# Centred norms of a two-block transformer kernel: the second tile's squares in two halves about the first half's mean

## The chip, the core and the metric

The kernel runs on one core of a Trainium2 chip. The core has a matmul engine (TensorE, PE), a vector engine (VectorE, DVE), an activation engine (ScalarE, ACT), a general engine (GpSimd, POOL) and a queue engine that issues DMAs (SyncE, SP). Each engine takes its own instructions in order; they meet only through semaphores. The metric is the device time of one execution in microseconds (us), lower is better.

## What is computed

Two model blocks on 256 tokens of width 1024, all in float32: a hybrid block (gated convolution and 16-head attention, between two RMS norms), then a two-layer block with memory attention, a sparse attention, another attention and two feed-forward nets. In the second block every sublayer ends in a layer norm of the scaled input plus the sublayer's output. It is this norm that the change touches:

```python
def layer_norm(x, g, b):
    xf = x.astype(jnp.float32)
    mu = xf.mean(-1, keepdims=True)
    var = jnp.square(xf - mu).mean(-1, keepdims=True)
    return ((xf - mu) * lax.rsqrt(var + LN_EPS) * g + b).astype(x.dtype)

        x = layer_norm(ALPHA * x + mix, ln1_g[layer], ln1_b[layer])
        ffn = conv_ffn(x, ffn_w_in[layer], ffn_conv_w[layer], ffn_conv_b[layer], ffn_w_out[layer])
        x = layer_norm(ALPHA * x + ffn, ln2_g[layer], ln2_b[layer])
```

## The kernel before

All weights come as one stream of 512 KB blocks (`raw`). SP loads them, ACT makes the rounded high part of each (`make_high`, L442, 128x1024), DVE the low part (`make_low`, L867), and PE multiplies the three products high*high, high*low and low*high. `ready(b)` on PE waits until the low part of block b is there (semaphore `split_l`). `refill(0, b)` on ACT and on DVE makes the parts of block b+3, once PE has used block b.

There are six norms, `n0` to `n5`. `n0` and `n1` are RMS norms; `n2`, `n3`, `n4` and `n5` are the centred ones. The 256 tokens are two tiles of 128 (t = 0 and 1). One norm goes like this:

- DVE (`norm_sum`): `add_up` (L927) adds the scaled residual and PE's sums, writes `z` and accumulates the row's total in `st`. Tile 0 is added in one piece of 1024 columns, and `mean(0, 1)` (L933) follows. Tile 1 is added in two halves of 512, since PE finishes its banks one after the other; then `mean(1, 2)` (L935) adds the two totals. A mean is kept negated in `st[:, 4+t]`.
- ACT (`norm_var`): for each tile one Square over 1024 columns with the negated mean as bias (L459); its accumulated total is the sum of squared deviations, `st[:, 6+t]`. The total is written by a separate accumulator read behind it, and that raises `var`. Between the two tiles stands `refill(0, soon)`, the high part of one weight block; `n5` has none.
- POOL (`rstd`): variance / 1024 + eps (L346), then the power -0.5 (L348), once for each tile.
- DVE: tile 0 is centred and scaled in two halves (L976), then `refill(0, soon)` makes the low part of the same weight block (L867), then tile 1 is centred and scaled (L976) and two more refills may follow (`n2` and `n3`; `n4` has none there).
- PE (`turn_x`, L1644) transposes each tile, from which ACT (`norm_high`, L472) and DVE (`norm_x`, L893, L879) make the next matmuls' operands.

What PE does meanwhile differs: at `n2` it multiplies `keys(0)` of the memory, `turn_x(0)`, the first half of `keys(1)`, `turn_x(1)`, the second half; `keys(1)` needs the block whose parts `soon` makes. At `n3` it multiplies one block for the memory's values, then waits for the `soon` block, then `turn_x(0)`, half of that block, `turn_x(1)`, the rest. At `n4` it has twelve matmuls on zeros, then both `turn_x`. `n5` is the end of the program: DVE centres and gains both tiles (L960), then scales and shifts both (L966, which needs POOL's `rstd`), and SP writes each tile out.

The order of every engine's instructions is written out by hand; no planner moves them. Inside `n2` to `n4` the critical lines are these:

```python
                for t in range(NT):
                    norm_wait(act, nm, "mean" if centred else "sum", t + 1)
                    if t:
                        norm_wait(act, nm, "var", t)
                    act.activation(sq[:, :], z[:, t, :], ACT.Square,
                                   bias=st[:, 4 + t:5 + t] if centred else 0.0,
                                   accum_out=st[:, 6 + t:7 + t]).then_inc(S[nm, "var"], 1)
                    if t == 0 and soon is not None:
                        refill(0, soon)
```

## Time and profile before

| | |
|---|---|
| median of 3 runs | 949.84 us (949.72 to 951.45) |
| the profiled execution, whole | 950.55 us |
| its span in the trace | 948.9 us |
| PE busy | 927.5 us, 98% |
| DVE busy | 664.6 us, 70% |
| ACT busy | 529.7 us, 56% |
| POOL busy | 66.6 us, 7% |

Times in the trace are us from the span's start. A row of a timeline gives the start, the time on the engine, the engine, the line, the operation, what it writes and reads, the shape, how many were merged (x2), and in square brackets the idle time of the engine just before it with what ended that time. Neighbouring rows of one engine can overlap by a little, since instructions are pipelined. The span of one execution and the whole of it differ by 1.65 us; a time before or after the change is compared with the median, and a shift that is worked out from the trace is added to the median.

### The profile page before, as it was taken

What the parts mean: (1) busy time and instruction counts of PE and PEld (TensorE: products, weight loads), DVE (VectorE), ACT (ScalarE), POOL (GpSimd) and SP (SyncE); (2) the same over time, 40 slices, a digit from 0 to 9 for tenths busy, and PEclk for the clock granted to TensorE, in tenths of its full rate; (3) what the DMA queues carried; (4) which work ended last, traced back from release to release, by engine and by line L of the source; (5) the groups of instructions that cost most, each with busy time, mean ns of one, the idle gap of its engine ahead of it and who ended that gap; (6) DMA issues with size and microseconds to landing.
All of it is one profiled execution on the core that took longest, in us unless ns stands there. A gap on an engine that the chain in (4) does not pass through costs nothing.

```text
span 948.9 us, 19737 instructions
## 1 busy us (share of the span) xinstructions
PE 927.5 (98%) x7030; PEld 845.8 (89%) x7030; DVE 664.6 (70%) x1286; ACT 529.7 (56%) x976; POOL 66.6 (7%) x116
## 2 busy tenths in 40 slices
PE   9999999999999999999999999999999999999995
PEld 6899999999999988767999999998988799999995
DVE  7666666666767877986886665667677796666666
ACT  6545555555554668763755554546665565555553
POOL 1000000000000002730000000001000100000001
PEclk9999999999999999999999999999999999999998
DMA  8565555557565675313566656555554456555541
GB/s 271 190 193 177 185 187 170 184 175 235 194 193 191 218 243 173 121 58 136 175 216 227 198 178 199 194 186 184 175 183 156 155 177 225 196 194 182 196 158 45
DMA packets 48235, 173.02 MB, mean 182 GB/s; under 512 B 6031, under 2 KB 6479, under 8 KB 48060
## 3 DMA queue, kind: packets, MB, share of 16 engines
q1 hardware_dynamic: 44732, 159.78, 51.5%
q0 software_dynamic: 3456, 12.61, 4.2%
q8 instruction: 30, 0.49, 0.2%
q14 instruction: 17, 0.14, 0.0%
HBM read 171.29 MB, written 1.07 MB: 182 GB/s over the span
## 4 chain that ended last, share of the span: by engine, by line
PE 89%; DVE 6%; ACT 3%; issue 2%; POOL 1%; POOLq 0%; DVEq 0%; ACTq 0%
PE bank L1534 18%; PE bank L1535 18%; PE bank L1533 18%; PE ysum L1604 6%; PE ysum L1606 6%; PE ysum L1605 6%; PE bank L1655 2%; DVE sb_wl L867 2%; PE ysum L1662 1%; PE ysum L1669 1%; ACT sb_xh L472 1%; PE ysum L1701 1%; PE ysum L1707 1%; PE ysum L1704 1%; PE ysum L1533 1%
## 5 line engine op out<-in xcount | busy, mean ns | idle before, releaser
L1534 PE MATMUL bank<-sb_xl,sb_wh 128*128 128x256 f32 x1360 | 378.2, 278 | 0.0
L1535 PE MATMUL bank<-sb_xh,sb_wl 128*128 128x256 f32 x1360 | 376.1, 277 | 0.0
L1533 PE MATMUL bank<-sb_xh,sb_wh 128*128 128x256 f32 x1332 | 370.7, 278 | 1.4 <-DVE sb_wl L867 1.4
L867 DVE TENSOR_TENSOR sb_wl<-sb_raw,sb_wh 128x1024 fp32r<-128x1024 f32 x201 | 245.5, 1223 | 103.6 <-ACT sb_wh L442 102.4
L442 ACT ACTIVATE sb_wh<-sb_raw 128x1024 fp32r<-128x1024 f32 x201 | 211.0, 1054 | 84.1 <-PE ysum L1606 36.3
L1533 PEld LDWEIGHTS bank<-sb_xh,sb_wh 128*128 128x128 f32 x1332 | 250.1, 188 | 6.4 <-issue 4.4
L1535 PEld LDWEIGHTS bank<-sb_xh,sb_wl 128*128 128x128 f32 x1360 | 255.7, 188 | 0.0
L1534 PEld LDWEIGHTS bank<-sb_xl,sb_wh 128*128 128x128 f32 x1360 | 255.5, 188 | 0.0
L867 DVE TENSOR_TENSOR sb_wl<-sb_gates,sb_wh 128x1024 fp32r<-128x1024 f32 x66 | 80.6, 1221 | 18.5 <-ACT sb_wh L442 18.4
L1605 PE MATMUL ysum<-sb_wl,sb_mh 128*128 128x512 f32 x208 | 81.1, 390 | 0.0
L1606 PE MATMUL ysum<-sb_wh,sb_ml 128*128 128x512 f32 x208 | 81.0, 390 | 0.0
L1604 PE MATMUL ysum<-sb_wh,sb_mh 128*128 128x512 f32 x208 | 81.0, 389 | 0.0
L442 ACT ACTIVATE sb_wh<-sb_gates 128x1024 fp32r<-128x1024 f32 x66 | 69.7, 1057 | 15.5 <-PE bank L1535 7.3
L764 ACT ACTIVATE sb_t_a<-bank,sb_convf 128x256 f32<-128x256 f32 x44 | 24.9, 566 | 71.1 <-PE bank L1535 68.6
L484 ACT ACTIVATE sb_pr<-sb_sc,sb_mx 128x128 f32<-128x128 f32 x80 | 35.4, 444 | 24.5 <-DVE sb_mx L1014 24.5
L1431 DVE SCALAR_TENSOR_TENSOR sb_t_a<-bank,sb_convf,sb_t_a 128x255 f32<-128x255 f32 x44 | 21.2, 483 | 39.5 <-ACT sb_t_a L764 39.4
L867 DVE TENSOR_TENSOR sb_wl<-sb_t_dg,sb_wh 128x1024 fp32r<-128x1024 f32 x33 | 40.4, 1224 | 12.0 <-ACT sb_wh L442 12.0
L1606 PEld LDWEIGHTS ysum<-sb_wh,sb_ml 128*128 128x128 f32 x208 | 39.0, 188 | 8.2
L1604 PEld LDWEIGHTS ysum<-sb_wh,sb_mh 128*128 128x128 f32 x208 | 39.0, 188 | 7.4
L1605 PEld LDWEIGHTS ysum<-sb_wl,sb_mh 128*128 128x128 f32 x208 | 39.0, 188 | 7.1
L442 ACT ACTIVATE sb_wh<-sb_t_dg 128x1024 fp32r<-128x1024 f32 x33 | 35.0, 1060 | 10.2 <-PE bank L1535 5.4
L774 ACT ACTIVATE sb_mh<-sb_t_c 128x256 fp32r<-128x256 f32 x44 | 18.0, 409 | 33.7 <-PE ysum L1606 33.5
(296 smaller groups left out, 1492.7 us busy)
## 6 DMA issues: line engine op xcount, KB each, us to landing
sb_raw<-in_stream SPq DMA_DIRECT2D x201, 512.0 KB, 3.4
sb_gates<-in_stream SPq DMA_DIRECT2D x66, 512.0 KB, 3.5
sb_t_dg<-in_stream SPq DMA_DIRECT2D x33, 512.0 KB, 4.2
sb_bias<-rel_rows POOLq DMA_DIRECT2D x12, 384.0 KB, 4.2
sb_bias<-in_alibi POOLq DMA_DIRECT2D x8, 256.0 KB, 3.1
sb_gb<-in_ln_g POOLq DMA_DIRECT2D x4, 512.0 KB, 4.7
sb_gb<-in_ln_b POOLq DMA_DIRECT2D x4, 512.0 KB, 6.7
sb_x_tok<-in_x SPq DMA_DIRECT2D x2, 512.0 KB, 3.8
```

The source lines that it names most:

```text
L442: act.activation(wh[slot_of(b)][:, :, :], raw[home_of(b)][:, :, :], ACT.Copy).then_inc(split_h, 1)
L484: act.activation(to[:, branch, h, cols], src, ACT.Exp, bias=mx[:, c:c + 1], scale=-1.0, accum_out=den[:, c:c + 1]).then_inc(S[ph, "exp"], 1)
L764: act.activation(t_a[:, :], bank[2 * c][:, 0:T], ACT.Identity, bias=convf[:, layer, bass.ds(i, 1), 3], scale=convf[:, layer, bass.ds(i, 1), 2]
L867: dve.tensor_tensor(wl[slot_of(b)][:, :, :], raw[home_of(b)][:, :, :], wh[slot_of(b)][:, :, :].bitcast(F32), ALU.subtract).then_inc(split_ ...
L1431: cf.link(dve.scalar_tensor_tensor(out=t_a[:, 1:T], in0=bank[2 * c][:, 0:T - 1], scalar=convf[:, layer, bass.ds(i, 1), 1], in1=t_a[:, 1:T] ...
L1533: pe.matmul(out, wh[slot][:, k, :], mov_h(k), start=k == 0, stop=False)
L1534: pe.matmul(out, wh[slot][:, k, :], mov_l(k), start=False, stop=False)
L1535: last = pe.matmul(out, wl[slot][:, k, :], mov_h(k), start=False, stop=k == KT - 1)
L1604: pe.matmul(out, th[:, t * P:(t + 1) * P], hw, start=start, stop=False)
L1605: pe.matmul(out, th[:, t * P:(t + 1) * P], lw, start=False, stop=False)
L1606: last = pe.matmul(out, tl[:, t * P:(t + 1) * P], hw, start=False, stop=stop)
L1655: last = pe.matmul(outs[h][:, cols], q[r, t * P:(t + 1) * P], k[r, 0:lead + (t + 1) * P], start=True, stop=True)
```

## The change

For tile 1 of the four centred norms the variance is taken in another way. Let m1 be the mean of the first 512 columns. DVE writes -m1/32 into `st[:, 3]` right behind the first half's add and raises `sum`. ACT then takes the Square in two halves of 512 columns, both about m1 and scaled by 1/32, so that the two totals (`st[:, 7]`, `st[:, 13]`) add up to the mean of (z - m1)^2. The first half needs only the first half's add; it raises `half_var`. The second waits for the second half's add and raises `var`. Since both are about m1 and not about the tile's mean, DVE computes the correction (mean - m1)^2 in three more 128x1 instructions behind `mean(1, 2)`; the last of the three also takes the first half's total, so it waits for `half_var`, and it raises `rest`. POOL waits for `var` and `rest` and adds the two parts (with eps already in, and eps as a floor). Tile 0, and the RMS norms, stay as they were. Six unused semaphores of the phase `p2` go.

```diff
@@ -239,10 +239,10 @@
         S = {}
 
         norms = ["n0", "n1", "n2", "n3", "n4", "n5"]
-        per_norm = {"sum": 2, "mean": 2, "var": 2, "rstd": 2, "z": 4, "x": 2, "half": 2, "off": 2,
+        per_norm = {"sum": 2, "mean": 2, "var": 2, "rstd": 2, "z": 4, "x": 2, "half": 2, "off": 2, "half_var": 1, "rest": 1,
                     "turned": KT, "xf": 6, "xf_act": 2, "xh": KT, "xl": KT}
 
-        first_norm = {"sum": 1, "mean": 2, "x": 1, "half": 1, "off": 2}
+        first_norm = {"sum": 1, "mean": 2, "x": 1, "half": 1, "off": 2, "half_var": 2, "rest": 2}
         for what in per_norm:
             one = sem(f"norm_{what}")
             for nm in norms:
@@ -269,7 +269,10 @@
         for what in ("xc", "tz", "yc", "yc_h", "ta", "ya", "ya_h"):
             S["p1", what] = sem(f"p1_{what}")
         for ph in ("p2", "f0", "f1"):
-            for what in ("free_a", "m", "mh", "ml", "base", "g"):
+            for what in ("free_a", "m", "mh", "ml"):
+                S[ph, what] = sem(f"{ph}_{what}")
+        for ph in ("f0", "f1"):
+            for what in ("base", "g"):
                 S[ph, what] = sem(f"{ph}_{what}")
         v_pair, prc_clear = sem("v_pair"), sem("prc_clear")
         v_up = [sem("v1_up"), sem("v2_up")]
@@ -343,8 +346,12 @@
             def rstd(nm, t, eps):
 
                 norm_wait(pool, nm, "var", t + 1)
-                chain.link(pool.tensor_scalar(st[:, 8 + t:9 + t], st[:, 6 + t:7 + t], 1.0 / D, eps,
-                                              ALU.mult, ALU.add))
+                if t and norms.index(nm) > 1:
+                    norm_wait(pool, nm, "rest", 1)
+                    chain.link(pool.tensor_scalar(st[:, 9:10], st[:, 13:14], st[:, 14:15], eps, ALU.add, ALU.max))
+                else:
+                    chain.link(pool.tensor_scalar(st[:, 8 + t:9 + t], st[:, 6 + t:7 + t], 1.0 / D, eps,
+                                                  ALU.mult, ALU.add))
                 pool.tensor_tensor(st[:, 10 + t:11 + t], st[:, 8 + t:9 + t], half[:, :],
                                    ALU.pow).then_inc(S[nm, "rstd"], 1)
 
@@ -453,6 +460,15 @@
             def norm_var(nm, centred, soon=None):
 
                 for t in range(NT):
+                    if t and centred:
+                        norm_wait(act, nm, "var", t)
+                        for n, total in ((0, 7), (1, 13)):
+                            norm_wait(act, nm, "sum", n + 1)
+                            part = slice(n * D // 2, (n + 1) * D // 2)
+                            act.activation(sq[:, part], z[:, t, part], ACT.Square, bias=st[:, 3:4], scale=1.0 / 32,
+                                           accum_out=st[:, total:total + 1]
+                                           ).then_inc(S[nm, "var" if n else "half_var"], 1)
+                        continue
                     norm_wait(act, nm, "mean" if centred else "sum", t + 1)
                     if t:
                         norm_wait(act, nm, "var", t)
@@ -945,11 +961,23 @@
                     ins.then_inc(S[nm, "sum"], 1)
                 norm_wait(dve, nm, "half", 2)
                 chain.link(add_up(1, slice(0, D // 2), 2))
+                if centred:
+                    dve.tensor_scalar(st[:, 3:4], st[:, 2:3], -1.0 / (16 * D), None, ALU.mult
+                                      ).then_inc(S[nm, "sum"], 1)
                 dve.wait_ge(used, last_block + 1)
                 ins = add_up(1, slice(D // 2, D), 1)
                 if centred:
-                    chain.link(ins)
+                    ins.then_inc(S[nm, "sum"], 1)
+                    norm_wait(dve, nm, "sum", 2)
                     mean(1, 2)
+                    norm_wait(dve, nm, "mean", 2)
+                    chain.link(dve.scalar_tensor_tensor(out=st[:, 12:13], in0=st[:, 5:6], scalar=1.0 / 32,
+                                                        in1=st[:, 3:4], op0=ALU.mult, op1=ALU.subtract))
+                    chain.link(dve.scalar_tensor_tensor(out=st[:, 15:16], in0=st[:, 12:13], scalar=-1.0 * D,
+                                                        in1=st[:, 12:13], op0=ALU.mult, op1=ALU.mult))
+                    norm_wait(dve, nm, "half_var", 1)
+                    dve.scalar_tensor_tensor(out=st[:, 14:15], in0=st[:, 7:8], scalar=EPS_LN, in1=st[:, 15:16],
+                                             op0=ALU.add, op1=ALU.add).then_inc(S[nm, "rest"], 1)
                 else:
                     ins.then_inc(S[nm, "sum"], 1)
                 if nm == "n5":
```

DVE around norm `n4`, before (`sb_z` is the tensor normed, `sb_st` the statistics, `sb_wl` the low part of a weight block, `dve_chain` DVE's waits for itself):

```order
L927 SCALAR_TENSOR_TENSOR sb_z,sb_st<-sb_x_tok,ysum 128x512 [waits norm_half]
L927 SCALAR_TENSOR_TENSOR sb_z,sb_st<-sb_x_tok,ysum 128x512 [waits used,dve_chain]
L935 TENSOR_SCALAR sb_st<-sb_st 128x1 [waits dve_chain]
L976 TENSOR_SCALAR sb_z<-sb_z,sb_st 128x512 [waits norm_mean,norm_rstd]
L976 TENSOR_SCALAR sb_z<-sb_z,sb_st 128x512
L867 TENSOR_TENSOR sb_wl<-sb_raw,sb_wh 128x1024 [waits split_h]
L976 TENSOR_SCALAR sb_z<-sb_z,sb_st 128x512 [waits norm_mean,norm_rstd]
```

and the same place now:

```order
L943 SCALAR_TENSOR_TENSOR sb_z,sb_st<-sb_x_tok,ysum 128x512 [waits norm_half]
L965 TENSOR_SCALAR sb_st<-sb_st 128x1 [waits dve_chain]
L943 SCALAR_TENSOR_TENSOR sb_z,sb_st<-sb_x_tok,ysum 128x512 [waits used]
L951 TENSOR_SCALAR sb_st<-sb_st 128x1 [waits norm_sum]
L974 SCALAR_TENSOR_TENSOR sb_st<-sb_st 128x1 [waits norm_mean]
L976 SCALAR_TENSOR_TENSOR sb_st<-sb_st 128x1 [waits dve_chain]
L979 SCALAR_TENSOR_TENSOR sb_st<-sb_st 128x1 [waits norm_half_var,dve_chain]
L1004 TENSOR_SCALAR sb_z<-sb_z,sb_st 128x512 [waits norm_mean,norm_rstd]
L1004 TENSOR_SCALAR sb_z<-sb_z,sb_st 128x512
L883 TENSOR_TENSOR sb_wl<-sb_raw,sb_wh 128x1024 [waits split_h]
L1004 TENSOR_SCALAR sb_z<-sb_z,sb_st 128x512 [waits norm_mean,norm_rstd]
```

Three instructions now stand between the mean and tile 0's scaling, one of them with a wait for ACT, and a fourth stands between the two adds. `n2` and `n3` read the same.

ACT around norm `n4`, before (`sb_pr` takes the squares, which nobody reads; `sb_wh` is the high part of a weight block):

```order
L459 ACTIVATE sb_pr,sb_st<-sb_z,sb_st 128x1024 [waits norm_mean]
L442 ACTIVATE sb_wh<-sb_raw 128x1024 [waits landed1,used]
L459 ACTIVATE sb_pr,sb_st<-sb_z,sb_st 128x1024 [waits norm_var,norm_mean]
L442 ACTIVATE sb_wh<-sb_raw 128x1024 [waits landed2,used]
L472 ACTIVATE sb_xh<-ysum,sb_gbt 128x256 [waits norm_turned] x4
```

and now:

```order
L475 ACTIVATE sb_pr,sb_st<-sb_z,sb_st 128x1024 [waits norm_mean]
L449 ACTIVATE sb_wh<-sb_raw 128x1024 [waits landed1,used]
L468 ACTIVATE sb_pr,sb_st<-sb_z,sb_st 128x512 [waits norm_sum,norm_var]
L468 ACTIVATE sb_pr,sb_st<-sb_z,sb_st 128x512 [waits norm_sum]
L449 ACTIVATE sb_wh<-sb_raw 128x1024 [waits landed2,used]
L488 ACTIVATE sb_xh<-ysum,sb_gbt 128x256 [waits norm_turned] x4
```

One Square has become two, both still behind the high part of the `soon` block.

DVE at the end of the program, `n5`, before:

```order
L927 SCALAR_TENSOR_TENSOR sb_z,sb_st<-sb_x_tok,ysum 128x512 [waits used,dve_chain]
L935 TENSOR_SCALAR sb_st<-sb_st 128x1 [waits dve_chain]
L960 SCALAR_TENSOR_TENSOR sb_x_tok<-sb_z,sb_st,sb_gb 128x1024 [waits norm_mean,gb_in]
L960 SCALAR_TENSOR_TENSOR sb_x_tok<-sb_z,sb_st,sb_gb 128x1024 [waits norm_mean]
L966 SCALAR_TENSOR_TENSOR sb_x_tok<-sb_x_tok,sb_st,sb_gb 128x1024 [waits norm_rstd,norm_off] x2
```

and now:

```order
L943 SCALAR_TENSOR_TENSOR sb_z,sb_st<-sb_x_tok,ysum 128x512 [waits used]
L951 TENSOR_SCALAR sb_st<-sb_st 128x1 [waits norm_sum]
L974 SCALAR_TENSOR_TENSOR sb_st<-sb_st 128x1 [waits norm_mean]
L976 SCALAR_TENSOR_TENSOR sb_st<-sb_st 128x1 [waits dve_chain]
L979 SCALAR_TENSOR_TENSOR sb_st<-sb_st 128x1 [waits norm_half_var,dve_chain]
L988 SCALAR_TENSOR_TENSOR sb_x_tok<-sb_z,sb_st,sb_gb 128x1024 [waits norm_mean,gb_in]
L988 SCALAR_TENSOR_TENSOR sb_x_tok<-sb_z,sb_st,sb_gb 128x1024 [waits norm_mean]
L994 SCALAR_TENSOR_TENSOR sb_x_tok<-sb_x_tok,sb_st,sb_gb 128x1024 [waits norm_rstd,norm_off] x2
```

The same three instructions now stand ahead of the four long ones that write the output.

## Rows read from the trace of the kernel before

**Rows 1.** The page's chain that ended last, shares by engine.
```profile
PE 89%; DVE 6%; ACT 3%; issue 2%; POOL 1%; POOLq 0%; DVEq 0%; ACTq 0%
```

**Rows 2.** Timeline of DVE at norm n4: start us, us, engine, line, instruction.
```profile
751.66 0.08 DVE L927 DVE_READ_ACCUMULATOR sb_z<-sb_x_tok,ysum 128x1 f32 x1
751.78 0.21 DVE L935 TENSOR_SCALAR sb_st<-sb_st 128x1 f32<-128x1 f32 x1
751.97 1.00 DVE L976 TENSOR_SCALAR sb_z<-sb_z,sb_st 128x512 f32<-128x512 f32 x2
752.89 1.22 DVE L867 TENSOR_TENSOR sb_wl<-sb_raw,sb_wh 128x1024 fp32r<-128x1024 f32 x1
754.82 1.00 DVE L976 TENSOR_SCALAR sb_z<-sb_z,sb_st 128x512 f32<-128x512 f32 x2 [0.72 <-POOL sb_st L348]
```

**Rows 3.** Timeline of ACT at norm n4.
```profile
750.91 1.04 ACT L442 ACTIVATE sb_wh<-sb_raw 128x1024 fp32r<-128x1024 f32 x1
752.03 1.15 ACT L459 ACTIVATE sb_pr<-sb_z,sb_st 128x1024 f32<-128x1024 f32 x1
753.09 0.19 ACT L459 ACTIVATION_READ_ACCUMULATOR sb_pr<-sb_z,sb_st 128x1 f32 x1
```

**Rows 4.** Timeline of POOL at norm n4: tile 0, then tile 1.
```profile
751.10 0.18 POOL L346 TENSOR_SCALAR sb_st<-sb_st 128x1 f32<-128x1 f32 x1 [2.14 <-ACT sb_pr L459]
751.37 0.56 POOL L348 TENSOR_TENSOR sb_st<-sb_st,sb_half 128x1 f32<-128x1 f32 x1
753.36 0.80 POOL L346 TENSOR_SCALAR sb_st<-sb_st 128x1 f32<-128x1 f32 x1 [1.43 <-ACT sb_pr L459]
```

**Rows 5.** Timeline of PE at norm n4, tile 1's transposes.
```profile
755.42 1.11 PE L1644 MATMUL ysum<-sb_ident,sb_z 128*128 128x128 f32 x8 [1.00 <-DVE sb_z L976]
```

**Rows 6.** Groups of ACT instructions by line and shape: count, busy us, mean ns, idle before.
```profile
L484 ACT ACTIVATE sb_pr<-sb_sc,sb_mx 128x256 f32<-128x256 f32 x40 | 19.8, 495 | 0.0
L459 ACT ACTIVATE sb_pr<-sb_z,sb_st 128x1024 f32<-128x1024 f32 x8 | 9.2, 1152 | 17.1 <-DVE sb_st L933 15.8 <-DVE sb_st L935 1.0
```

**Rows 7.** Timeline of DVE, two small instructions, the second waiting for the first.
```profile
370.30 0.18 DVE L1331 RECIPROCAL sb_rden<-sb_deng 128x4 f32<-128x4 f32 x1
370.51 0.17 DVE L1334 TENSOR_TENSOR sb_rg<-sb_rden,sb_g_nsa 128x4 f32<-128x4 f32 x1
```

**Rows 8.** Timeline of DVE, then PE, at norm n2.
```profile
453.95 1.22 DVE L867 TENSOR_TENSOR sb_wl<-sb_t_dg,sb_wh 128x1024 fp32r<-128x1024 f32 x1
...
455.48 0.36 PE L1533 MATMUL bank<-sb_memh,sb_wh 128*128 128x256 f32 x1
...
465.92 0.35 PE L1533 MATMUL bank<-sb_xh,sb_wh 128*128 128x256 f32 x1 [0.73 <-DVE sb_wl L867]
```

**Rows 9.** Timeline of DVE, then PE, at norm n3.
```profile
643.75 1.22 DVE L867 TENSOR_TENSOR sb_wl<-sb_raw,sb_wh 128x1024 fp32r<-128x1024 f32 x1
...
645.03 0.87 PE L1644 MATMUL bank<-sb_ident,sb_z 128*128 128x128 f32 x6 [0.42 <-DVE sb_wl L867]
...
656.32 0.50 PE L1581 MATMUL ysum<-sb_wh,sb_xh 128*128 128x512 f32 x1 [0.98 <-DVE sb_wl L867]
```

**Rows 10.** Timeline at norm n5, the program's end: DVE, ACT, POOL.
```profile
940.36 2.47 DVE L960 SCALAR_TENSOR_TENSOR sb_x_tok<-sb_z,sb_st,sb_gb 128x1024 f32<-128x1024 f32 x2
942.75 1.28 DVE L966 SCALAR_TENSOR_TENSOR sb_x_tok<-sb_x_tok,sb_st,sb_gb 128x1024 f32<-128x1024 f32 x1
944.57 1.28 DVE L966 SCALAR_TENSOR_TENSOR sb_x_tok<-sb_x_tok,sb_st,sb_gb 128x1024 f32<-128x1024 f32 x1 [0.54 <-POOL sb_st L348]
...
940.48 1.15 ACT L459 ACTIVATE sb_pr<-sb_z,sb_st 128x1024 f32<-128x1024 f32 x1 [1.00 <-DVE sb_st L935]
...
941.80 1.07 POOL L346 TENSOR_SCALAR sb_st<-sb_st 128x1 f32<-128x1 f32 x1 [1.40 <-ACT sb_pr L459]
942.96 1.47 POOL L348 TENSOR_TENSOR sb_st<-sb_st,sb_half 128x1 f32<-128x1 f32 x1
```

**Rows 11.** DVE's low parts: count, duration ns min/median/max, first and last start us.
```profile
L867 DVE TENSOR_TENSOR sb_wl<-sb_raw,sb_wh x201: 1202/1225/1228, 8.9 to 924.6; 128x1024 fp32r<-128x1024 f32 x101
```

## The prediction

> **What bounds the kernel now.** First the page's chain: 89% of the span is PE [rows 1]. A change to the norms counts only where PE waits for one. Then the timelines at the four centred norms, read backwards from PE's idle time. The cleanest is `n4`: PE sits idle 1.00 us ahead of tile 1's transposes [rows 5], because DVE sat idle 0.72 us ahead of tile 1's scaling, waiting for POOL's rstd [rows 2]. Behind that stand ACT's Square and the weight block's high part ahead of it [rows 3]. The delay goes on through ACT's and DVE's operands into the next matmuls, and nothing later gives it back, as PE bounds the long stretches. At `n2` PE waits 0.73 us at 465.92 for a low part made at the end of DVE's unbroken row of work since tile 1's scaling [rows 8]. At `n3` PE waits 0.42 us ahead of tile 0's transposes for the low part of the `soon` block, and 0.98 us at 656.32 for a later one [rows 9]. At `n5` the last DVE instruction waits 0.54 us for rstd and ends the program [rows 10].
>
> **ACT's part, n2 to n4.** The change lets the first half square start after the first half's add. At `n4` that would be near 751.2, but ACT is busy with the weight block's high part, which starts at 750.91 and takes 1.04 [rows 3]; the next could start at about 751.86. Before, the Square began at 752.03, when the mean (751.78 + 0.21, [rows 2]) had landed. So the earlier start is worth about 0.15, not a whole half. Two halves cost more than one whole: 128x256 with bias and accumulation takes 495 ns, 128x1024 takes 1152 [rows 6]; on the line between them 512 columns take about 0.71 us (bounds 0.58, half of 1152, and 0.80), and the next follows about 0.70 after. First half 751.86, second 752.56; its accumulator read ends 1.50 after the first start, at 753.36. Before, 753.09 + 0.19 = 753.28 [rows 3]. `var` comes **0.08 later**, not earlier. The first half's total, which raises `half_var`, lands 0.80 after its start, at 752.66.
>
> **DVE's part, n2 to n4.** The -m1/32 ahead of the second add costs about 0.10 (the row for the like mean is 0.15 to 0.21 long, and part overlaps). The second add's total therefore lands at 751.84 instead of 751.74 [rows 2]. Then the mean, and two 128x1 instructions that each wait for the one ahead: dependent small instructions follow each other at 0.21 [rows 7], so the last of the new ones could start at 752.50. But it waits for `half_var`, at 752.66, so it starts near 752.70 and tile 0's scaling near 752.82 instead of 751.97: **0.85 later** (0.67 if the wait did not bind). Queued behind the waiting instruction are tile 0's scaling, the `soon` low part (752.89 becomes about 753.74, ending 754.96) and tile 1's scaling. Who waits for them: PE, for tile 0's scaling at `turn_x(0)`, and for that low part at `n2` and `n3`.
>
> **POOL's part.** POOL's first instruction takes 0.18 undisturbed (tile 0) but 0.80 for tile 1 at `n4`: it started at 753.36 and ended at 754.16, 0.05 after DVE's low part, which read two SBUF tensors from 752.89 to 754.11 [rows 2, 4]. At `n5` the power started at 942.96 under such a DVE instruction and took 1.47, ending 0.40 after it, against 0.56 undisturbed [rows 4, 10]. So a POOL instruction that wants to read while a two-input DVE instruction runs stands still until it ends. The Trainium skill's page "SBUF — State Buffer", section "SBUF: two separate sides", says that DVE (with two SBUF inputs) and GpSimd take an exclusive lock on a shared port pair, and whoever starts first has it for the whole instruction. By that rule the trace agrees when DVE is first; when POOL is first, no row here shows it.
>
> After the change, POOL's first instruction would start at 753.36 + 0.08 = 753.44. It now runs beside tile 0's scaling, which reads one tensor, so I take it as undisturbed: 0.18, perhaps 0.1 more for its second operand. The power then starts 0.27 to 0.37 after it, at 753.71 to 753.81 and reads some 0.1 later. The low part starts at 753.74. This is nearly a tie, and decides 0.5 us: the blockage has moved from POOL's first instruction to its second. I take the power as blocked, since its read lies behind the low part's start at most values. Then rstd lands at 754.96 + 0.40 = 755.36, and tile 1's scaling starts near 755.42 instead of 754.82.
>
> **The sum.**
> - `n4`: tile 1's scaling **+0.61** (blocked), +0.10 if the power is in time, because then the scaling follows the low part's end in DVE's own order. PE, ACT and DVE all follow from it.
> - `n2`: the same pattern, with the low part from 453.95 to about 454.83. PE's `keys(1)` at 455.48 needs it; it would end at 456.05, so PE starts 0.6 later. But that part of the delay runs into the 0.73 idle at 465.92. DVE's chain from tile 1's scaling decides: **+0.58** (blocked), +0.10 in time.
> - `n3`: the low part starts at 643.75 + 0.88 = 644.63, and PE's tile 0 transposes, which waited for it, move from 645.03 to 645.91. Tile 1's transposes, ACT's operands and DVE's follow; the idle 0.98 at 656.32 is the end of that same chain, so it hides nothing. **+0.87** in either case.
> - `n5`: ACT is free, idle 1.00 ahead of its Square at 940.48 [rows 10], so the first half is hidden, and the second starts with the second add's total, about 0.1 before 940.48. It is 0.44 shorter than the whole (1.15 - 0.71), so `var` lands 0.55 earlier, and POOL could start at 941.25 instead of 941.80. But the four long DVE instructions start after the new small ones, at 941.08 instead of 940.36 [rows 10], 0.72 later. Back to back their last starts 0.72 - 0.54 = 0.18 later, the 0.54 being its idle wait. But POOL starts inside the first of them and the power inside the second, which ends near 943.55, so rstd comes 0.40 after it at about 943.95, in time for the last one. **+0.2**, bounds 0.1 and 0.4.
>
> Together 0.61 + 0.58 + 0.87 + 0.2 = 2.26, or +0.24%. The profiled execution took 950.55, 0.71 above the median 949.84; I add the shift to the median: **952.1**. The other edits (fewer semaphores, POOL's maximum in place of a multiply, the longer wait lists) I cost at nothing: a semaphore that nobody waits for has no row, and POOL is busy 7%.
>
> **The rivals.**
> 1. *The power is in time* at `n2` and `n4`. For it: the tie is within 0.1 us, and faster halves (0.65 instead of 0.70) decide it. Against: POOL's instruction has gained an operand. 0.10 + 0.10 + 0.87 + 0.2 = 1.27, so **951.1**. One of the two in time gives 951.6.
> 2. *POOL is first and DVE waits for it.* The `soon` low part would start only when the power ends, at `n4` near 754.3, and tile 1's scaling near 755.45. At `n3` the low part would start about 645.15 instead of 643.75, which is 1.4 for PE; `n2` and `n4` give 0.6 each, `n5` 0.3: 2.9, so **952.7**. Against it: 201 low parts all last between 1.20 and 1.23 us [rows 11], so none was held up once it had started. The skill's page "SBUF — State Buffer" states this direction too, as the lock is held by whoever started first; by that rule the sum is this 2.9.
> 3. *The change does what it says, and is faster.* Place: tile 1's scaling at `n2` to `n4`. Its 0.72 idle would vanish if rstd came 0.7 earlier and DVE's queue were held up by less than that. The price would be 0.5 for each of three norms, and 0.4 at `n5`: -1.9, **947.9**. It decides at the start of tile 0's scaling: unless that moves by under 0.2, the queue eats the gain. Against: the small instructions alone make 0.67, and ACT cannot begin the half before 751.86.
>
> **How the numbers follow.** 50% for the forecast (its own range 951.5 to 952.8), 29% for rival 1 with its mixed form, 12% for rival 2, 3% for rival 3, and 6% that the delay is mostly given back downstream (950.2 or so). A measurement of this kernel can tell about 0.2%, 1.9 us, from no change: the line is at 951.74, between the forecast and rival 1. Slower by over 0.2%: 0.8 of the forecast, rival 2 and a little of rival 1, 0.54. Faster: 0.03. Within: 0.43. The runs of before spread over 1.7 us, so 0.5 is added on either side of the cases: 950.6 to 953.3.
>
> **What would show it.** In the profile of the changed kernel: the two 512-column squares about 0.7 long and adjoining; at `n2` to `n4` DVE idle or waiting for ACT ahead of the last new small instruction, and tile 0's scaling 0.8 to 0.9 further from the second add than before; POOL's first instruction 0.2 to 0.3 long, its power about 1.5 long (0.56 in rival 1); PE's idle 0.42 at `n3` grown to 1.3; at `n5` no idle time between the four long DVE instructions. I am wrong if tile 0's scaling moves by less than 0.5, if 512 columns take under 0.6, or if the waits of later stages take the delay in.

## The result, and the profile after

| | before | after |
|---|---|---|
| median of 9 runs | 950.23 us (949.38 to 951.45) | 954.42 us (953.12 to 956.31) |
| the profiled execution, whole | 950.55 us | 954.74 us |
| its span in the trace | 948.9 us | 953.1 us |

The ratio is 1.0045, interval 1.0036 to 1.0053: the change makes the kernel 4.2 us slower. The direction was forecast, the size was not: 2.3 us were expected, and 954.42 lies above the range's 953.3. (The forecast stood on a median of 949.84 for the kernel before, which is 0.4 less than the 950.23 here; the rest of the miss is the change's own.)

The page of the kernel after, its busy times and its chain that ended last (before: [rows 1]):

```profile
PE 929.0 (97%) x7025; PEld 846.6 (89%) x7030; DVE 666.2 (70%) x1302; ACT 530.5 (56%) x984; POOL 68.6 (7%) x116
...
PE 87%; DVE 6%; ACT 3%; issue 2%; POOL 1%; DMA 1%; DVEq 0%; SPq 0%; ACTq 0%
```

PE's share of the chain has gone from 89% to 87%. The rest is at the four norms. `n4` first, DVE's timeline from tile 1's mean to its scaling (before: [rows 2]):

```profile
754.04 0.21 DVE L951 TENSOR_SCALAR sb_st<-sb_st 128x1 f32<-128x1 f32 x1
754.29 0.16 DVE L974 SCALAR_TENSOR_TENSOR sb_st<-sb_st 128x1 f32<-128x1 f32 x1
754.48 0.16 DVE L976 SCALAR_TENSOR_TENSOR sb_st<-sb_st 128x1 f32<-128x1 f32 x1
754.99 0.16 DVE L979 SCALAR_TENSOR_TENSOR sb_st<-sb_st 128x1 f32<-128x1 f32 x1 [0.34 <-ACT sb_pr L468]
755.10 1.00 DVE L1004 TENSOR_SCALAR sb_z<-sb_z,sb_st 128x512 f32<-128x512 f32 x2
756.01 1.22 DVE L883 TENSOR_TENSOR sb_wl<-sb_raw,sb_wh 128x1024 fp32r<-128x1024 f32 x1
757.99 1.00 DVE L1004 TENSOR_SCALAR sb_z<-sb_z,sb_st 128x512 f32<-128x512 f32 x2 [0.76 <-POOL sb_st L355]
```

ACT, POOL and PE at the same place (before: [rows 3 to 5]):

```profile
754.08 0.71 ACT L468 ACTIVATE sb_pr<-sb_z,sb_st 128x512 f32<-128x512 f32 x1
...
754.79 0.71 ACT L468 ACTIVATE sb_pr<-sb_z,sb_st 128x512 f32<-128x512 f32 x1
```
```profile
755.69 1.62 POOL L351 TENSOR_SCALAR sb_st<-sb_st 128x1 f32<-128x1 f32 x1 [1.52 <-ACT sb_pr L468]
757.40 0.56 POOL L355 TENSOR_TENSOR sb_st<-sb_st,sb_half 128x1 f32<-128x1 f32 x1
```
```profile
758.59 1.54 PE L1672 MATMUL ysum<-sb_ident,sb_z 128*128 128x128 f32 x8 [1.78 <-DVE sb_z L1004]
...
760.36 0.41 PE L1574 MATMUL bank<-sb_xh,sb_wh 128*128 128x256 f32 x1
...
762.76 0.28 PE L1574 MATMUL bank<-sb_xh,sb_wh 128*128 128x256 f32 x1
```

Three readings. First, DVE sits 0.34 us in front of L979 and waits for ACT's first half; tile 0's scaling starts 0.90 us later than before, both counted from the first half's add, which starts at 752.52 here and at 750.29 before (0.85 was expected). Second, POOL's first instruction lasts 1.62 us. It starts at 755.69, inside the second half of tile 0's scaling (which ends at 756.10) and 0.32 ahead of the low part at 756.01, and ends at 757.31, 0.08 behind that low part's end at 757.23. The power runs only then, undisturbed in 0.56, and ends at 757.96. DVE, waiting 0.76, starts tile 1's scaling at 757.99. Third, PE's idle time ahead of tile 1's transposes has grown from 1.00 to 1.78 us, and its matmuls behind it are long: transposes 1.54 in place of 1.11, then 0.41 in place of 0.28 for 128x256, until about 762.5. The windows of that stretch (us, busy time and count of PE, PEld, DVE, ACT, POOL, then the granted clock, DMA share, GB/s):

```profile
752.50:758.50 6.00, 4.24 (x22) 2.13 (x22) 4.74 (x14) 4.04 (x8) 2.94 (x4) 1.00 0.41 129
758.50:762.50 4.00, 3.91 (x21) 3.86 (x22) 3.25 (x9) 3.43 (x8) 0.00 (x0) 0.58 0.34 122
762.50:766.50 4.00, 4.00 (x35) 4.00 (x35) 3.87 (x9) 1.23 (x3) 0.00 (x0) 1.00 0.01 4
```

The granted clock is 0.58 in the middle one. With the short instructions back from 762.5, PE stood at its lower level, 1.2 GHz, for some 3.4 us (759.1 to 762.5). In the kernel before, the two like stretches (751.5 to 757.5 and to 761.5) are granted 1.00.

What this cost is read best at the low part of `sb_gates` just behind it; first the changed kernel, then the kernel before:

```profile
768.40 1.23 DVE L883 TENSOR_TENSOR sb_wl<-sb_gates,sb_wh 128x1024 fp32r<-128x1024 f32 x1
...
763.97 1.23 DVE L867 TENSOR_TENSOR sb_wl<-sb_gates,sb_wh 128x1024 fp32r<-128x1024 f32 x1
```

It starts 10.41 us behind tile 1's scaling here (757.99) and 9.15 before (754.82): **1.26 us** for the clock. Further on the two traces come 0.4 closer again, and that is no gain of the change: between 775 and 785 the trace of before loses 0.4 of its own, as only one of the other ten traces does (the correction behind tile 0's scaling).

At `n2` and `n3` the same pattern stands, without the clock. DVE, POOL and PE there (before: [rows 8, 9]):

```profile
455.08 1.22 DVE L883 TENSOR_TENSOR sb_wl<-sb_t_dg,sb_wh 128x1024 fp32r<-128x1024 f32 x1
```
```profile
454.76 1.64 POOL L351 TENSOR_SCALAR sb_st<-sb_st 128x1 f32<-128x1 f32 x1 [1.53 <-ACT sb_pr L468]
```
```profile
467.10 0.36 PE L1561 MATMUL bank<-sb_xh,sb_wh 128*128 128x256 f32 x1 [0.72 <-DVE sb_wl L883]
...
647.00 0.88 PE L1672 MATMUL bank<-sb_ident,sb_z 128*128 128x128 f32 x6 [1.32 <-DVE sb_wl L883]
...
658.33 0.50 PE L1609 MATMUL ysum<-sb_wh,sb_xh 128*128 128x512 f32 x1 [1.04 <-DVE sb_wl L883]
```

At the end of the program, `n5` (before: [rows 10]):

```profile
945.04 2.49 DVE L988 SCALAR_TENSOR_TENSOR sb_x_tok<-sb_z,sb_st,sb_gb 128x1024 f32<-128x1024 f32 x2
947.46 2.47 DVE L994 SCALAR_TENSOR_TENSOR sb_x_tok<-sb_x_tok,sb_st,sb_gb 128x1024 f32<-128x1024 f32 x2
```
```profile
945.40 1.10 POOL L351 TENSOR_SCALAR sb_st<-sb_st 128x1 f32<-128x1 f32 x1 [0.94 <-ACT sb_pr L468]
946.58 1.37 POOL L355 TENSOR_TENSOR sb_st<-sb_st,sb_half 128x1 f32<-128x1 f32 x1
```

The four long ones now stand without idle time between them.

Where the 4.2 us came in, each from the same instruction in both traces, with what the two traces already differed by at that norm's first half add taken off:

| place | expected | measured |
|---|---|---|
| ahead of `n2` (no change there) | 0 | 0.22 |
| `n2`, by PE at 467.10 (465.92 before) | 0.58 | 0.96 |
| `n3`, by PE at 647.00 and 658.33 | 0.87 | 0.90, later 0.94 |
| `n4`, tile 1's scaling | 0.61 | 0.94 |
| `n4`, from there to `n5`'s first add: PE at its lower level (1.26), less the 0.4 of the trace of before | not foreseen | 0.88 |
| `n5`, to the span's end | 0.2 | 0.1 |

That is 4.04 us with `n3` at 0.94; the rest is spread between the places. The 0.22 ahead of `n2` is scatter: the like add lies between 0.67 earlier (the kernel without the change at `n4`) and 1.60 later (the one with it at `n5` alone) in the other traces. So two things were missing: about 0.35 at each of `n2` and `n4`, and 1.26 by the clock.

### The profile page after: what moved, and what is told of

It is laid out like the page before. It is cut to its first block, busy times and chain, and to the rows that moved or that the text cites. A ratio compares the mean times of both kernels' runs of the same rounds, so it can differ in the third digit from the quotient of the medians.

```text
span 953.1 us, 19760 instructions
## 1 busy us (share of the span) xinstructions
PE 929.0 (97%) x7025; PEld 846.6 (89%) x7030; DVE 666.2 (70%) x1302; ACT 530.5 (56%) x984; POOL 68.6 (7%) x116
## 3 DMA queue, kind: packets, MB, share of 16 engines
HBM read 171.29 MB, written 1.07 MB: 181 GB/s over the span
## 4 chain that ended last, share of the span: by engine, by line
PE 87%; DVE 6%; ACT 3%; issue 2%; POOL 1%; DMA 1%; DVEq 0%; SPq 0%; ACTq 0%
PE bank L1562 18%; PE bank L1563 18%; PE bank L1561 18%; PE ysum L1632 6%; PE ysum L1634 6%; PE ysum L1633 6%; DVE sb_wl L883 2%; PE bank L1683 2%; PE ysum L1690 1%; PE ysum L1697 1%; ACT sb_wh L449 1%; PE ysum L1729 1%; PE ysum L1735 1%; PE ysum L1732 1%; PE ysum L1561 1%
```

## The experiments

Several kernels share their runs of the kernel before, and each ratio below is to those. Theory A, formed from the trace of after: POOL's first instruction, with a column as its second operand and beside tile 0's scaling, still wants to read when the low part starts, and is caught; the power then runs undisturbed behind it. Its rivals: the power alone would be late anyway; DVE's row of small instructions is all of it; the clock at `n4` has another cause.

### POOL's first instruction with constants only

```diff
-                    chain.link(pool.tensor_scalar(st[:, 9:10], st[:, 13:14], st[:, 14:15], eps, ALU.add, ALU.max))
+                    chain.link(pool.tensor_scalar(st[:, 9:10], st[:, 13:14], 1.0, eps, ALU.mult, ALU.add))
```

The variance of tile 1 then lacks its correction and the first half's total.

> The changed kernel, but POOL's first instruction for tile 1 takes 1.0 and eps as constants instead of the column of the correction; it still waits for the same semaphores. So the correction and the first half's total are left out of the variance. Theory A (the new instruction with a second operand column lasts about 0.34 us, as the like 128x15 rows do, and so runs into DVE's low part; with constants it lasts 0.18): the first instruction reads in time, 0.18 long; the power behind it either is caught (ends 0.4 after the low part) or just gets in. Tile 1's scaling comes 0.3 to 0.7 earlier than in the changed kernel at n2 and n4, n3 stays, and PE's clock drop at n4 may go: 950.2 + 1.3 to 3.1. Theory B (POOL is caught there whatever its operands, since DVE reads and writes the same statistics tile beside it): the first instruction still lasts 1.6, total as the changed kernel, 954.

952.39 us, ratio 1.0027 (1.0017 to 1.0037), 2.3 over before and 2.0 under the changed kernel. `n4` in its trace, POOL, DVE and PE:

```profile
754.57 0.47 POOL L351 TENSOR_SCALAR sb_st<-sb_st 128x1 f32<-128x1 f32 x1 [1.52 <-ACT sb_pr L468]
755.12 1.42 POOL L355 TENSOR_TENSOR sb_st<-sb_st,sb_half 128x1 f32<-128x1 f32 x1
```
```profile
753.99 1.00 DVE L1004 TENSOR_SCALAR sb_z<-sb_z,sb_st 128x512 f32<-128x512 f32 x2
754.90 1.22 DVE L883 TENSOR_TENSOR sb_wl<-sb_raw,sb_wh 128x1024 fp32r<-128x1024 f32 x1
756.57 1.00 DVE L1004 TENSOR_SCALAR sb_z<-sb_z,sb_st 128x512 f32<-128x512 f32 x2 [0.45 <-POOL sb_st L355]
```
```profile
757.17 1.11 PE L1672 MATMUL ysum<-sb_ident,sb_z 128*128 128x128 f32 x8 [1.47 <-DVE sb_z L1004]
```

This is the course that the prediction had taken: POOL's first instruction gets through (0.47), the power is caught and ends at 756.54, 0.42 behind the low part's end, and the scaling waits 0.45 in place of 0.76. The sum of that course was +2.26, and +2.3 was measured. PE idles 1.47 and its transposes take 1.11: the clock stays. The one operand decides both misses.

But the first instruction does not take 0.18 to 0.28 here either. It ends at 755.04, 0.05 behind the end of tile 0's scaling (753.99 + 1.00 = 754.99), although the low part has begun by then. The same holds wherever constants are used. Beside the scaling it ends 0.05 behind a scaling half in all nine places (`n2` to `n4` of this kernel, of the three small instructions alone, and of the low part first), whether it started 0.26 or 0.42 ahead of that end. Beside the low part, in the kernel before, it also ends 0.05 behind. So the one-tensor scaling holds POOL as the two-input low part does, only for a shorter time: 512 columns take 0.55. What the constants gain is that the instruction gets through between the scaling and the low part, where the one with the column does not.

### The correction left out

The three small instructions and `rest` go; POOL waits for `half_var` and adds the two totals. The variance is then about m1 and not about the tile's mean.

```diff
-                    norm_wait(pool, nm, "rest", 1)
-                    chain.link(pool.tensor_scalar(st[:, 9:10], st[:, 13:14], st[:, 14:15], eps, ALU.add, ALU.max))
+                    norm_wait(pool, nm, "half_var", 1)
+                    chain.link(pool.tensor_scalar(st[:, 9:10], st[:, 13:14], st[:, 7:8], eps, ALU.add, ALU.add))
```

> ACT's part alone: the two half squares about the first mean stay, DVE's three small instructions and their wait go, POOL adds the two totals. The correction by the squared distance of the means is left out. Theory A (the loss comes from the small instructions held in DVE's queue and what POOL then runs into): tile 1's scaling +0.1 at n2 and n4, n3 +0.1, n5 earlier by 0.4: total 0.2 under the kernel before, within noise of it, and no clock drop. Rival (the halves themselves cost: two fixed costs on ACT, the later total): 0.5 or more over before.

950.84 us, ratio 1.0009 (1.0000 to 1.0018), +0.7. That is nearer to the rival (0.5 or more over before) than to theory A (0.2 under). Without DVE's row, the halves alone give nothing back at `n2` to `n4` either: POOL's first instruction takes 0.80 to 0.82 there, since it starts with the low part running, as before, and tile 1's scaling comes 0.13 later than before. A gain of 0.4 was expected at `n5`, and did not come:

```profile
941.39 1.61 POOL L351 TENSOR_SCALAR sb_st<-sb_st 128x1 f32<-128x1 f32 x1 [0.94 <-ACT sb_pr L468]
943.08 1.45 POOL L355 TENSOR_TENSOR sb_st<-sb_st,sb_half 128x1 f32<-128x1 f32 x1
```
```profile
944.66 1.28 DVE L986 SCALAR_TENSOR_TENSOR sb_x_tok<-sb_x_tok,sb_st,sb_gb 128x1024 f32<-128x1024 f32 x1 [0.55 <-POOL sb_st L355]
```

`var` came earlier, but both of POOL's instructions were caught by DVE's long ones, and the last of these waits 0.55 as it did before (0.54). An earlier release is worth only as much as lets POOL read in an earlier gap of DVE. So the halves do not help even alone.

### The same three instructions in the kernel before

They stand in the same place and depend on each other in the same way; the last one has no wait for ACT, and nobody reads their results.

```diff
@@ norm_sum of the kernel before, behind mean(1, 2)
+                    norm_wait(dve, nm, "mean", 2)
+                    chain.link(dve.scalar_tensor_tensor(out=st[:, 12:13], in0=st[:, 5:6], scalar=1.0 / 32,
+                                                        in1=st[:, 5:6], op0=ALU.mult, op1=ALU.subtract))
...
```

> DVE's part alone: the kernel before with three dependent 128x1 instructions behind the second mean of each centred norm; their results are read by nobody, and there is no wait for ACT. Theory A: tile 0's scaling and the soon low part start 0.55 later at n2, n3 and n4. At n3 PE waits that long. At n2 and n4 POOL's first instruction for tile 1 now starts beside the scaling, just ahead of the low part. If it is caught by it, tile 1's scaling comes 0.6 later, and the total is 1.8 over before; if it reads in time and the power is caught, 0.3 later and 1.2 over. n5: 0. Rival (small instructions are free, since DVE then waits 0.72 for rstd anyway): 0 to 0.3 over before.

951.93 us, ratio 1.0019 (1.0009 to 1.0028), +1.8: DVE's row alone, with nothing of ACT's or POOL's changed, makes four tenths of the change's 4.2. POOL at `n4`:

```profile
754.66 0.31 POOL L346 TENSOR_SCALAR sb_st<-sb_st 128x1 f32<-128x1 f32 x1 [1.43 <-ACT sb_pr L459]
755.05 1.41 POOL L348 TENSOR_TENSOR sb_st<-sb_st,sb_half 128x1 f32<-128x1 f32 x1
```

With constants the first instruction starts 0.17 ahead of the low part (754.83) and is in time all the same. Against 0.18 undisturbed [rows 4] it takes 0.31, since it waits for the end of the scaling: that runs from 753.91 to 754.91, and the instruction ends at 754.97.

### The column operand alone, in the kernel before

```diff
-                chain.link(pool.tensor_scalar(st[:, 8 + t:9 + t], st[:, 6 + t:7 + t], 1.0 / D, eps,
-                                              ALU.mult, ALU.add))
+                if norms.index(nm) > 1:
+                    chain.link(pool.tensor_scalar(st[:, 8 + t:9 + t], st[:, 6 + t:7 + t], 1.0 / D,
+                                                  st[:, 4 + t:5 + t], ALU.mult, ALU.max))
+                else:
...
```

In the centred norms eps is left out here.

> The kernel before, with one operand of POOL's first instruction in the centred norms taken from a statistics column instead of a constant (the larger of the variance and the negated mean; eps is left out). Theory A: for tile 0, where nothing disturbs it, the instruction lasts 0.34 instead of 0.18, as the 128x15 rows with such an operand do; for tile 1 it is caught by the low part as before, 0.80. Total within 0.2 of before. Rival (the operand costs nothing): 0.18 for tile 0, same total.

951.36 us, ratio 1.0013 (1.0003 to 1.0022). Tile 0 of `n4`, undisturbed, then tile 1 of `n5`:

```profile
751.78 0.30 POOL L347 TENSOR_SCALAR sb_st<-sb_st 128x1 f32<-128x1 f32 x1 [2.16 <-ACT sb_pr L463]
...
942.36 2.29 POOL L347 TENSOR_SCALAR sb_st<-sb_st 128x1 f32<-128x1 f32 x1 [1.31 <-ACT sb_pr L463]
```

The operand costs 0.12 undisturbed (0.30 against 0.18, [rows 4]); at tile 1 of `n2` to `n4`, caught by the low part, the instruction is 1.03 to 1.05 long in place of 0.80. It now ends 0.16 behind the low part (0.05 before), and the low part itself is 0.14 later, since tile 0's scaling waits for a later rstd: together tile 1's scaling comes 0.27 later at each of the three. At `n5` the instruction had not got through when the next long DVE instruction began, and was held to its end as well, 2.29 against 1.07 [rows 10]: theory A's mechanism at another place. DVE's last instruction ends 0.32 later there, counted from the first half's add. So the +1.2, where 0.2 at most were expected, comes from all four norms.

### The correction behind tile 0's scaling

The three instructions are moved as they are, at `n2` to `n4`, to stand between tile 0's scaling and the `soon` low part:

```diff
+                    if t == 0 and centred:
+                        correction()
                     if t == 0 and soon is not None:
                         refill(0, soon)
```

> The changed kernel with the three small instructions behind tile 0's scaling and ahead of the soon low part at n2 to n4, so that the scaling isn't held. Theory A: tile 0's scaling only 0.1 later than before, but the low part 0.6 later, and the rest lands as the low part starts, so POOL is caught for its whole length: tile 1's scaling 0.7 over before, n3 0.65, total 2.0 over before, with the chance of PE's clock drop at n4 0.9 more. Rival (the hold of tile 0's scaling is what costs): total within 1 of before.

952.49 us, ratio 1.0026 (1.0016 to 1.0036), +2.4. Tile 0's scaling is back in its place, but POOL now waits for `rest` in DVE's row and starts when the low part is already running:

```profile
754.32 1.22 DVE L883 TENSOR_TENSOR sb_wl<-sb_raw,sb_wh 128x1024 fp32r<-128x1024 f32 x1
756.38 1.00 DVE L1008 TENSOR_SCALAR sb_z<-sb_z,sb_st 128x512 f32<-128x512 f32 x2 [0.84 <-POOL sb_st L355]
```
```profile
754.58 1.12 POOL L351 TENSOR_SCALAR sb_st<-sb_st 128x1 f32<-128x1 f32 x1 [1.67 <-DVE sb_st L962]
```

Caught at 754.58, through at 755.70: 0.16 behind the low part's end. The correction costs DVE's time wherever it stands.

### The low part ahead of the last small instruction

```diff
+                    if soon is not None:
+                        refill(0, soon)
                     norm_wait(dve, nm, "half_var", 1)
...
-                    if t == 0 and soon is not None:
+                    if t == 0 and soon is not None and not centred:
                         refill(0, soon)
```

> The changed kernel, with the soon low part made ahead of the last of the three small instructions and of tile 0's scaling at n2 to n4. Theory A: no two-input instruction follows tile 0's scaling, so POOL's first instruction shows its own length beside the scaling, with the second operand: 0.5 to 0.65 instead of 1.6; the power 0.6 to 0.75. Tile 1's scaling 0.5 over before at n4, n3 0.4, n2 0.5, no clock drop: total 1.2 to 1.6 over before, so more than 2 under the changed kernel. Rival (the instruction with two columns is 1.6 long by itself): no gain over the changed kernel.

952.09 us, ratio 1.0019 (1.0009 to 1.0028), +2.0, less gain than expected. POOL now meets only the one-tensor scaling (`n4`, then `n2`):

```profile
754.85 0.44 POOL L351 TENSOR_SCALAR sb_st<-sb_st 128x1 f32<-128x1 f32 x1 [1.98 <-DVE sb_st L981]
...
454.77 0.77 POOL L351 TENSOR_SCALAR sb_st<-sb_st 128x1 f32<-128x1 f32 x1 [2.00 <-DVE sb_st L981]
```

1.62 has become 0.44 at `n4`, and 1.64 has become 0.77 at `n2`. So the low part was what held it longest; but the scaling holds it too. At `n2` and `n3` the instruction ends 0.03 behind the scaling's second half (455.51 and 645.91), at `n4` 0.15 behind its first half (755.14), and the power there, 0.63 long, ends 0.43 behind the second. At all three it starts 0.26 behind the scaling's start; why it gets through between the halves at one norm and not at the other two stays open.

### The clock: filler between the transposes

```diff
                 turn_x("n4", t)
+                if t == 0:
+                    warm_up(6)
```

Six matmuls on zeros keep PE busy between tile 0's and tile 1's transposes; nothing else differs from the changed kernel.

> The changed kernel with six matmuls on zeros between the two tiles' transposes at n4, about 1.4 us inside PE's 1.78 us of idle time. Theory C (after the longer idle time PE is granted half its clock for 3.4 us, which costs about 0.9 of the 4.2): the granted clock stays whole through 755 to 770, matmuls of 128x256 behind the transposes take 0.28 and not 0.41, total 0.9 under the changed kernel, about 953.5. Rival (the clock drop is hidden behind DVE's chain, or the 0.9 comes from elsewhere): same total as the changed kernel.

953.63 us (4 runs), ratio 1.0041 (1.0026 to 1.0056). PE at `n4`:

```profile
756.27 1.46 PE L1707 MATMUL bank<-sb_zeros 128*128 128x512 bf16 x6
758.22 1.11 PE L1672 MATMUL ysum<-sb_ident,sb_z 128*128 128x128 f32 x8 [0.49 <-DVE sb_z L1004]
```
```profile
758.00:762.00 4.00, 3.71 (x30) 3.47 (x31) 3.47 (x9) 3.31 (x8) 0.00 (x0) 1.00 0.37 128
```

POOL and DVE run as in the changed kernel (1.62 and 0.76), yet the transposes take 1.11 and the clock is whole. The low part of `sb_gates` is back where it was:

```profile
766.75 1.22 DVE L883 TENSOR_TENSOR sb_wl<-sb_gates,sb_wh 128x1024 fp32r<-128x1024 f32 x1
```

It starts 9.14 us behind tile 1's scaling (757.61), against 10.41 in the changed kernel and 9.15 before. In the times it is 0.8 us, and the two intervals overlap, so the price of the clock, 1.26, rests on the traces. Nor does each execution seem to pay it: among the nine of the changed kernel, four have a mean clock of 0.995 (954.35 to 956.31 us, median 954.98), the profiled one among them, and five have 0.996 to 0.998 (953.12 to 954.61, median 953.58, the level of the kernel with filler). With five of nine spared anyway, four executions with filler that are all spared would prove little by themselves. What speaks for the idle time is the other kernels: of their 90 executions only one has 0.995, and it belongs to the correction behind tile 0's scaling, where PE idles 1.59 (954.98 us; the other nine there 951.50 to 953.56).

### The change at three norms, and at the last one only

```diff
-                    if t and centred:
+                    if t and nm in ('n2', 'n3', 'n5'):
```

with the same condition in DVE's and POOL's part; the other has `'n5'` alone.

> The change at n2, n3 and n5 only; n4 as before (three bare semaphore increments stand behind its scaling to keep the counts). Theory A with C (each of n2 and n3 costs 0.9, n4 0.9 by its wait and 0.9 by PE's halved clock behind it, n5 nothing): 1.9 over before, 1.8 to 2.3 under the changed kernel, and a whole clock through n4. Rival (the costs aren't local: a later stage pays for n4 or takes it in): less than 1 under the changed kernel.

> The change at n5 only, n2 to n4 as before (three bare semaphore increments behind the scaling of each keep the counts). Theory A: the four long instructions of DVE run without idle time, as in the changed kernel, the last one ends 0.1 later: total within 0.3 of before. Rival (the tail pays for the small instructions in full, 0.6 or more): 950.8 or more.

Without `n4`: 952.37 us, ratio 1.0021 (1.0011 to 1.0030). So `n4` alone makes about half, 2.1 of the 4.2; the traces have 0.94 for the wait and 1.26 for the clock there, 2.20. PE's transposes at `n4` are as they were:

```profile
756.70 1.11 PE L1679 MATMUL ysum<-sb_ident,sb_z 128*128 128x128 f32 x8 [1.01 <-DVE sb_z L1007]
```

With `n5` alone: 950.93 us, ratio 1.0007 (0.9997 to 1.0016). The interval holds nothing at all as well as the 0.6 of the rival, so the times decide nothing here; in the trace DVE's last instruction ends 0.03 later than before, counted from tile 1's first half add, and that speaks for theory A.

### A version that beats both: the low part first

If the low part is what holds POOL, it should run before POOL needs to read. In the kernel before, without any of the change:

```diff
+                if soon is not None:
+                    refill(0, soon)
                 for t in range(NT):
...
-                    if t == 0 and soon is not None:
-                        refill(0, soon)
```

> The kernel before with one line moved: DVE makes the low part of the soon block ahead of tile 0's scaling instead of behind it, at n1 to n4. Theory A (POOL's tile 1 instructions are held by the two-input low part and not by the one-input scaling): POOL's first instruction lasts 0.18 instead of 0.80, tile 1's scaling comes 0.6 earlier at n2 and n4; n3 gains 0.4, n1 0.3 or so: 1.5 to 2.0 under the kernel before. Rival (any DVE work holds POOL, or tile 0's transposes, now 1.1 later, cost PE as much as it gains): no change, or 0.5 slower.

949.05 us (11 runs, 948.57 to 949.79), ratio 0.9989 (0.9980 to 0.9998). `n4`, DVE, POOL and PE:

```profile
751.01 1.23 DVE L867 TENSOR_TENSOR sb_wl<-sb_raw,sb_wh 128x1024 fp32r<-128x1024 f32 x1
752.15 0.99 DVE L978 TENSOR_SCALAR sb_z<-sb_z,sb_st 128x512 f32<-128x512 f32 x2
753.59 1.00 DVE L978 TENSOR_SCALAR sb_z<-sb_z,sb_st 128x512 f32<-128x512 f32 x2 [0.45 <-POOL sb_st L348]
```
```profile
752.39 0.35 POOL L346 TENSOR_SCALAR sb_st<-sb_st 128x1 f32<-128x1 f32 x1 [1.43 <-ACT sb_pr L459]
752.82 0.73 POOL L348 TENSOR_TENSOR sb_st<-sb_st,sb_half 128x1 f32<-128x1 f32 x1
```
```profile
752.75 1.12 PE L1644 MATMUL ysum<-sb_ident,sb_z 128*128 128x128 f32 x8 [0.17 <-DVE sb_z L978]
754.19 1.11 PE L1644 MATMUL ysum<-sb_ident,sb_z 128*128 128x128 f32 x8 [0.33 <-DVE sb_z L978]
```

POOL's first instruction falls from 0.80 to 0.35, and PE idles 0.17 + 0.33 = 0.50 around tile 0's and tile 1's transposes in place of 1.00. More was expected (1.5 to 2.0), on the ground that the one-input scaling would not hold POOL, and it does: the first instruction ends at 752.74, 0.05 behind the scaling's first half, and the power, 0.73 in place of 0.56, at 753.55, 0.41 behind its second. Tile 0's transposes are later, too, which PE had in time before. Each norm gains some 0.2 to 0.26; in all 1.1 us, and the interval excludes 1 by a hair.

## Why the prediction was right in its direction and too small

**ACT's part: right.** 512 columns take 0.71 (expected 0.71), the next follows 0.71 on (0.70), and `var` brings no gain.

**DVE's part: right.** DVE waited for `half_var` ahead of the last small instruction, and tile 0's scaling moved by 0.90 (0.85).

**POOL's part: the failed step.** The prediction took POOL's first instruction, beside the one-tensor scaling, "as undisturbed: 0.18, perhaps 0.1 more for its second operand", and saw the tie one instruction too late, at the power. It took 1.62. It starts 0.32 ahead of the low part. Against that stand 0.18 with constants undisturbed, 0.30 with a column (the kernel with the column operand alone), 0.31 to 0.47 with constants beside the scaling, and 0.44 or 0.77 with both (the low part ahead of the last small instruction). The premise that a one-tensor scaling leaves POOL undisturbed was wrong: the scaling holds the instruction to its end as well. With constants it then gets through behind the scaling; with the column it does not, and is held until 0.08 behind the low part's end, and the whole power (0.56) then stands behind that, where a caught power ends 0.42 behind it. So tile 1's scaling comes 757.99 - 757.23 = 0.76 behind the low part's end, and not 756.57 - 756.12 = 0.45: 0.31 more at `n4`, and the like at `n2`. The case that was not thought of was the one in which both of POOL's instructions are late; the kernel with constants ran the case that was, at +2.3. Even there the first instruction took 0.47 and not 0.18; the sum came out all the same, by luck, since the power behind it was caught in either case.

**The rule of who starts first.** The prediction named the Trainium skill's page "SBUF — State Buffer", section "SBUF: two separate sides": whichever of DVE's two-input operation and GpSimd's starts first holds the shared ports, and the other waits. The rows now show only one side of it. DVE running first holds POOL, up to 2.29 us. POOL started 0.32 ahead of the low part by its row and was the one held; the low part took 1.22 as ever. But it had started inside the scaling, which held it, and the low part followed the scaling without a gap, so POOL was not first and this doesn't speak against the rule. A start in a row can't be used to say who is first. The same section counts only a DVE operation with two SBUF inputs, or in its two-port mode, as one that takes the lock; by it the one-tensor scaling would cost POOL something only if it ran in that mode. The rows have 0.31 to 0.77 beside it against 0.18 or 0.30, and the ends of these rows show what takes the time: POOL is held to the end of a scaling half. That agrees with the rule if the scaling ran in that mode. No row names the mode; its columns do pass faster than the low part's, 512 of them in 0.46 us from one half to the next against 1024 in 1.13 between two adjoining low parts.

**The clock: a term that was missing.** That PE's idle time ahead of tile 1's transposes would grow, the sum said; it priced it at its length. From 1.00 to 1.78 us it also cost 1.26 behind it, at the lower level, in the trace and, it seems, in four of nine executions. Without the lost 0.31 the idle time is 1.47, and the clock stayed: the second miss hangs on the first.

**`n3` and `n2`: right in their paths.** At `n3` the tile 0 transposes decide, whatever POOL does: 0.90 measured, 0.87 expected. At `n2` DVE's chain from tile 1's scaling decides, as said, with the 0.96 of this longer wait.

**`n5`: too high by little.** The path was as said, with no idle time left between the long four. They start 0.63 later, counted from the first half's add (942.80, and 938.75 before), where 0.72 was expected, and the span ends 0.1 later, not 0.2 (DVE's last instruction 0.03). A part of it is the -m1/32 between the adds, which costs 0.05 and not 0.10.

**The rivals.** Rival 1 (power in time) did not occur in any run of the change. Rival 2 was nearest in size (+2.9), but not by its mechanism: no low part was held by POOL. Rival 3's condition, tile 0's scaling later by under 0.2, failed by 0.7; and the kernel without the correction shows that it would not have been enough, since POOL is caught by DVE even then. That last point was not in the prediction, which had priced rival 3 at -1.9. The range went wrong at its upper end: it had 0.5 for the runs' spread, nothing for a slower first instruction, although what a column operand costs on POOL had no row in it, and nothing for the clock.

## What to carry to other kernels

Price a small POOL instruction by the end of the DVE instruction that it meets, one-tensor scalings included, and not by its own length; then ask whether it gets through before the next one. Here one column operand made the difference, and it cost a whole DVE instruction. Two instructions in a row must both be checked. An instruction with a wait, put in an engine's queue to save time elsewhere, is paid by all that is queued behind it; here three 128x1 instructions cost 1.8 us alone, and the halves that they serve gained nothing even without them. Where a small result must get through, put the long DVE work ahead of the moment it is ready, and check whether a longer idle time of PE brings the lower clock with it.

## What the runs showed of the hardware that was not expected

- A 128x1 tensor_scalar on POOL takes 0.18 us with constants and 0.30 with a column as operand, and the power 0.56. Two of these times, 0.18 and 0.30, stand beside DVE's add of an SBUF and a PSUM operand, which does not hold them.
- DVE's one-tensor 128x512 scaling, SBUF to SBUF, holds POOL as a two-input instruction does. Behind the end of either, the tensor_scalar with constants ended 0.05 later and the power 0.40 to 0.43. With a column it ended 0.15 to 0.18 behind the instruction that it met, or was held by the next one too and ended 0.03 to 0.10 behind that (up to 2.29 us in all).
- PE's granted clock fell to its lower level, 1.2 GHz, for some 3.4 us after an idle time of 1.78 us, which cost 1.26 us; in the traces it did not after 1.59, 1.47 or 1.00 at the same place, nor after 1.66 at 387.5 in the kernel before.
